# Hybrid attention and short-convolution layer on one core: the last block's output in two halves, and the preparation of weights in other places

## The reference

```
n = RMSNorm(x) ; z = n @ W_in
A: gated linear attention, 4 heads, per-head RMSNorm, times silu(g)
B: cb * conv3(cc * cu), times silu(g_conv)
h = x + [A ; B] @ W_out
h = h + sigmoid(h @ W_g + b_g) * (p @ W_ple)
out = RMSNorm(h) * final_norm_w
```

## Time and profile before

| | |
|---|---|
| three runs | 2047.91, 2048.13, 2050.92 us |
| profiled execution, its own time | 2050.24 us |
| span of its trace | 2048.4 us |
| TensorE granted clock, mean | 0.99 of full speed |
| busy: PE, DVE, ACT, POOL | 97%, 65%, 38%, 34% |
| one load of a weight matrix on SP | 2048 KB, median 8.8 us from issue to landing |
| chain that ended last, by engine | PE 87%, DVE 5%, issue 3%, ACT 2%, DMA 1% |

### The profile page before, as it was taken

The page is one execution under the profiler, slowest core; times in us unless marked ns, Lnnn a source line. Parts: engine busy times, 40 slices in busy tenths (PEclk is TensorE's granted clock), DMA queues, the critical chain, the costliest instruction groups (busy, mean ns, idle before and its releaser), DMA issues.

```text
span 2048.4 us, 28892 instructions
## 1 busy us (share of the span) xinstructions
PE 1983.6 (97%) x11266; PEld 1722.9 (84%) x11266; DVE 1338.9 (65%) x1569; ACT 782.3 (38%) x1219; POOL 689.5 (34%) x758
## 2 busy tenths in 40 slices
PE   6999999999999879999999999999999999999996
PEld 4888888888888758888888888888788999999996
DVE  4775667666654365775775775685674577777776
ACT  4354354444433323323333233223223255445543
POOL 3766666666551131231331331255551000000000
PEclk9999999999999989999999999999999999999998
DMA  6345354354446232136532137585587812222222
GB/s 228 136 161 194 135 192 179 144 200 165 161 176 279 96 108 85 67 108 249 183 110 83 60 111 259 198 297 200 191 287 285 321 58 88 93 81 86 83 83 83
DMA packets 88305, 322.84 MB, mean 158 GB/s; under 512 B 11600, under 2 KB 22272, under 8 KB 77184
## 3 DMA queue, kind: packets, MB, share of 16 engines
q1 hardware_dynamic: 55328, 185.46, 24.6%
q0 software_dynamic: 32864, 135.85, 18.3%
HBM read 193.34 MB, written 127.93 MB: 157 GB/s over the span
## 4 chain that ended last, share of the span: by engine, by line
PE 87%; DVE 5%; issue 3%; ACT 2%; DMA 1%; POOL 0%; SPq 0%; DVEq 0%; ACTq 0%; POOLq 0%
PE bank L1220 14%; PE bank L1226 14%; PE bank L1222 14%; PE bank L966 8%; PE bank L974 8%; PE bank L967 8%; PE bank L1312 5%; PE bank L1306 5%; PE bank L1308 5%; PE bank L1053 1%; PE bank L1355 1%; PE bank L1354 1%; PE bank L1353 1%; PE bank L1113 1%; PE bank L1104 1%
## 5 line engine op out<-in xcount | busy, mean ns | idle before, releaser
L1220 PE MATMUL bank<-XH,WC 128*128 128x512 f32 x1344 | 526.2, 392 | 23.4 <-DVE ccs L2031 20.1
L1222 PE MATMUL bank<-XH,WC 128*128 128x512 f32 x1344 | 524.0, 390 | 0.0
L1226 PE MATMUL bank<-XL,WC 128*128 128x512 f32 x1344 | 523.9, 390 | 0.0
L2005 DVE TENSOR_TENSOR XL<-RQ,XH 128x1024 fp32r<-128x1024 f32 x168 | 220.9, 1349 | 244.6 <-ACT XH L1598 243.6
L1220 PEld LDWEIGHTS bank<-XH,WC 128*128 128x128 f32 x1344 | 253.1, 188 | 76.9 <-issue 20.8
L1226 PEld LDWEIGHTS bank<-XL,WC 128*128 128x128 f32 x1344 | 253.0, 188 | 52.7
L1222 PEld LDWEIGHTS bank<-XH,WC 128*128 128x128 f32 x1344 | 253.2, 188 | 52.0
L1312 PE MATMUL bank<-XLg,WC 128*128 128x256 f32 x896 | 254.2, 284 | 2.8 <-DVE XLg L2243 2.8
L1306 PE MATMUL bank<-XHg,WC 128*128 128x256 f32 x896 | 253.5, 283 | 0.0
L1308 PE MATMUL bank<-XHg,WC 128*128 128x256 f32 x896 | 253.4, 283 | 0.0
L1598 ACT ACTIVATE XH<-RQ 128x1024 fp32r<-128x1024 f32 x168 | 170.7, 1053 | 194.4 <-PE bank L1226 148.1
(11 more groups left out here) (216 smaller groups left out, 3651.4 us busy)
## 6 DMA issues: line engine op xcount, KB each, us to landing
WC<-w_scratch SPq DMA_DIRECT2D x28, 2048.0 KB, 8.8
RQ<-n_scratch POOLq DMA_DIRECT2D x32, 1024.0 KB, 5.4
w_scratch<-prep_hi POOLq DMA_DIRECT2D x84, 256.0 KB, 2.3
w_scratch<-PB POOLq DMA_DIRECT2D x84, 256.0 KB, 2.3
n_scratch<-raw SPq DMA_DIRECT2D x8, 2048.0 KB, 7.1
y_scratch<-y_sb SPq DMA_DIRECT2D x64, 256.0 KB, 2.8
RQ<-y_scratch POOLq DMA_DIRECT2D x16, 1024.0 KB, 5.7
xt<-xb_dram SPq DMA_DIRECT2D x64, 256.0 KB, 5.2
```

Source lines behind the costliest of these rows:

```text
L1220: nc.tensor.matmul(bank[:], WC[:, i, q, 0, k], xh, start=(k == 0 and i in (P1, P2, P5)), stop=False, skip_group_check=True)
L1222: nc.tensor.matmul(bank[:], WC[:, i, q, 1, k], xh, start=False, stop=False, skip_group_check=True)
L1226: mm = nc.tensor.matmul(bank[:], WC[:, i, q, 0, k], xl, start=False, stop=(k == 3), skip_group_check=True)
L2005: nc.vector.tensor_tensor(XL[:, k], RQ[:, OPERAND[s % 7], 2 * h:2 * h + 2], XH[:, k].bitcast(F32), ALU.subtract).then_inc(sx_lo, 1)
```

## The change

- **First product of a gate operand (`gate_product`).** For q = 0 the eight products with the high part come first, then the wait for the low part, then the four products with the low part. Before, the wait stood behind the second product.
- **Strips.** `STRIPS_OF` puts 0, 4, 4, 4, 3, 3, 3, 3 strips in steps 0 to 7.
- **Pieces.** `GATE_SLOTS` is now (1, 1, 1), (5, 3, 0), (5, 1, 1), (2) for steps 8 to 11. Before it was (1, 1, 1), (5, 3, 1), (5, 2, 1), and nothing in step 11.
- **Wait for weights.** Before P1's matrix of the gate stage SP waits for all strips and two of the stores' counters only, and for the rest before P5's. The wait for the `W_ple` tiles ahead of it stays.
- **Block 7.** P4 comes behind the per-layer products of units 6 and 7. The mean square is made apart for the two halves of the tokens (`last_stats`: fp32 products with ones over `acc` and, for units 6 and 7, over their squares directly), `last_rms` makes `Ln` and `Exp` of 256 tokens, `last_norm` scales 8 tiles of 256 tokens, t = 1 first, and SP stores each half in four transfers.

```diff
+LAST_STAT = (0, 5)
...
+STRIPS_OF = (0, 4, 4, 4, 3, 3, 3, 3)
...
-GATE_SLOTS = {NB: (1, 1, 1), NB + 1: (5, 3, 1), NB + 2: (5, 2, 1)}
+GATE_SLOTS = {NB: (1, 1, 1), NB + 1: (5, 3, 0), NB + 2: (5, 1, 1), NB + 3: (2,)}
...
                 if i == P1:
-                    wait_prepared(sp, g // NP + 2)
-                    if g == STEPS - 1:
+                    if g < STEPS - 1:
+                        wait_prepared(sp, g // NP + 2)
+                    else:
                         sp.wait_ge(tile_stored, 16 * 2 * STRIPS)
+                        sp.wait_ge(prep_stored[2], 16 * (24 + 8))
+                        sp.wait_ge(prep_stored[5], 16 * (84 + 14))
+                if i == P5 and g == STEPS - 1:
+                    wait_prepared(sp, 4)
...
-            store_out(NB - 1, 1)
+            for n, t in enumerate((1, 0)):
+                tokens = slice(t * HT, t * HT + HT)
+                for c in range(4):
+                    m = slice(2 * c, 2 * c + 2)
+                    sp.wait_ge(out_norm, 8 * (NB - 1 + n) + 2 * c + 2)
+                    sp.dma_start(out[NB - 1, :, m, tokens], raws[(NB - 1) % 2][:, m, tokens]).then_inc(rows_stored[c], 16)
...
                 if is_conv(g):
-                    for n in range(3 * g, 3 * g + 3):
+                    for n in range(sum(STRIPS_OF[:g]), sum(STRIPS_OF[:g + 1])):
                         strip(n)
-                elif g in GATE_SLOTS:
+                else:
                     gate_parts(g, 0)
-                elif g == STEPS - 1:
+                if g == STEPS - 1:
                     for n in range(PLE_K):
                         prep_tile(n)
...
-                        if q == 0 and k == 0:
-                            pe.wait_ge(gx_lo, z + 1)
-                        mm = nc.tensor.matmul(acc_ap, WC[:, i, q, 0, k], xl, start=False, stop=(k == 3),
-                                              skip_group_check=True)
+                        if q > 0:
+                            mm = nc.tensor.matmul(acc_ap, WC[:, i, q, 0, k], XLg[:, z % 2, k], start=False, stop=(k == 3),
+                                                  skip_group_check=True)
+                    if q == 0:
+                        pe.wait_ge(gx_lo, z + 1)
+                        for k in range(4):
+                            mm = nc.tensor.matmul(acc_ap, WC[:, i, q, 0, k], XLg[:, z % 2, k], start=False, stop=(k == 3),
+                                                  skip_group_check=True)
...
-                for c, i in enumerate((P2, P5, P3, P4)):
+                for c, i in enumerate((P2, P5, P3)):
                     gate_product(b, i)
                     ple_unit(b, 2 * c)
                     ple_unit(b, 2 * c + 1)
+                if b < NB - 1:
+                    gate_product(b, P4)
+                ple_unit(b, 6)
+                ple_unit(b, 7)
+                if b == NB - 1:
+                    gate_product(b, P4)
...
+            def last_stats():
...
+                pe.wait_ge(g_acc, 6 * b + 4)
+                product(1, acc[:, 1], True, True).then_inc(out_mean, 1)
+                pe.wait_ge(g_sum, 6 * b + 5)
+                product(0, acc[:, 0], True, False)
+                pe.wait_ge(g_sq, 8 * b + 7)
+                product(0, square_place(b, 6), False, False)
+                pe.wait_ge(g_sq, 8 * b + 8)
+                product(0, square_place(b, 7), False, True).then_inc(out_mean, 1)
...
+                if b == NB - 1:
+                    gate_square(b, 4)
+                    gate_square(b, 5)
+                    sigmoid(b, 6)
+                    gate_square(b, 6)
+                    sigmoid(b, 7)
+                    nc.scalar.preload_act_table_set(LOG_EXP)
+                    last_rms(1, NB)
+                    gate_square(b, 7)
+                    last_rms(0, NB + 1)
+                    return
...
+            for n, t in enumerate((1, 0)):
+                dve.wait_ge(out_rstd, NB + n)
+                last_norm(t)
```

More of the change, by code:

```diff
@@ L1373, in out_stats, with product @@
                     wait_out_read(STAT)
[L1374 to L1378 removed]
                 pe.wait_ge(out_split, b + 1)
                 mean_of_split(STAT, total_hi[:], total_lo[:]).then_inc(out_mean, 1)
+            def last_stats():
+                b = NB - 1
+                def product(t, squares, start, stop):
+                    bank = ps[LAST_STAT[t]][:, t * HT:t * HT + HT]
+                    for j in range(2):
+                        mm = nc.tensor.matmul(bank, ones[:].bitcast(F32), squares[:, j * HT:j * HT + HT],
+                                              start=(start and j == 0), stop=(stop and j == 1))
+                    return mm
+                pe.wait_ge(g_acc, 6 * b + 4)
[6 more added lines that the diff above has]
+                product(0, square_place(b, 7), False, True).then_inc(out_mean, 1)
             pe.wait_ge(memsets, 5)
@@ L1786, in gate, with last_rms @@
                 gate_square(b, 7)
+            def last_rms(t, n):
+                tokens = slice(t * HT, t * HT + HT)
+                act.wait_ge(out_mean, n)
+                nc.scalar.activation(R_out[:, tokens], ps[LAST_STAT[t]][:, tokens], ACT.Ln, bias=eps[:],
+                                     scale=1.0 / D_MODEL).then_inc(out_root, 1)
+                act.wait_ge(out_root, n)
+                nc.scalar.activation(R_out[:, tokens], R_out[:, tokens], ACT.Exp, scale=-0.5).then_inc(out_rstd, 1)
             def out_rms(b):
@@ L2333, in gate, with last_norm @@
                 gate_total(b)
+            def last_norm(t):
+                tokens = slice(t * HT, t * HT + HT)
+                for m in range(KT):
+                    here = raws[(NB - 1) % 2][:, m, tokens]
+                    nc.vector.scalar_tensor_tensor(out=here, in0=here, scalar=vec[:, V_FIN + m:V_FIN + m + 1],
+                                                   in1=R_out[:, tokens], op0=ALU.mult, op1=ALU.mult).then_inc(out_norm, 1)
             def final_norm(b, tiles):
```

20 lines of the change are left out of this document (5 added, 15 removed).

## The result

The changed kernel takes **2019.26 us** (median of four runs, 2017.04 to 2020.20) beside 2048.58 us of the kernel before in the same session. The ratio is 0.9853, 95% interval 0.9836 to 0.9870: 1.5% faster. The range (2010.0 to 2019.5) holds it, just; the forecast itself, 2012.4, is 6.9 us too low. The profiled execution took 2019.48 us with a span of 2017.7, where before it was 2048.4: 30.7 us less.

A forecast was written before the change was run, and what follows sets the result against it. PE, busy 97% of the span, was taken as the bound; its waits and the end were to give -22.5 - 5.0 + 0.5 - 3.9 - 4.8 = -35.7 us, from 2048.13 to 2012.4 us, range 2010 to 2019.5.

The forecast's parts named there:

- Strips out of step 0: Start of step 1: T1 no longer waits behind three strips, so PE's 20.1 us wait and slow restart go, -22.5 us.
- The fourth strips in steps 1 to 3: Steps 1 to 3: one more strip takes 6.7 us of POOL, covered by 18.31 us of idle time, 0 us.
- Piece 11 behind T3: Start of step 10: T3 and DVE get through earlier, so PE's 3.2 us wait and slow restart go, -5.0 us.
- Pieces 18 and 19: Step 11: W_ple tiles end about 10.4 us later, delaying the gate stage's loads and first low part, +0.5 us.
- rival 1: Step 11 gives some back: tiles outlast their cover or loads delay the first gate operand, 3 to 9 us, 2017; chance 0.17.
- a new wait of PE at the first gate products: Start of the gate stage: a new PE wait here, or at P5 of step 11, would show the prediction wrong.
- rivals 1 and 2: Step 11 gives some back, 0.17; PE's stall at step 10's start stays, 3 to 5 us, 2017, 0.12.
- The finer wait buys nothing: Ahead of P1's gate matrix: SP stands at the W_ple tiles first, so splitting the wait for weights gains nothing.
- High products first: P6 in gate blocks 1 to 7: six more products before the low-part wait remove 0.55 us seven times, -3.9 us.
- The last block: Kernel's end: scalings of two token halves end at 2040.5 instead of 2045.3, last store landing as before, -4.8 us.
- the first went whole: Start of step 1: a rival had the 20.1 us stall go only in part, 2018 to 2030; chance 0.06.
- stores were not served one by one: Kernel's end: a rival had eight stores go one by one at 2.7 us each, 2025; chance 0.04.

The follow-up runs named there:

- the one with the pieces back: The changed kernel with GATE_SLOTS as before the change, so no pieces in step 11 and piece 11 again ahead of T3: 2011.54 us.
- the pieces are done earlier: The changed kernel with GATE_SLOTS (2, 2, 1), (6, 1, 0), (5, 2, 1), (0) for steps 8 to 11: 2014.07 us, ratio 0.9828.
- first experiment: The changed kernel with SP's wait for the W_ple tiles and the p_raw load put behind the loads of P1's, P6's and P7's matrices: 2018.67 us, ratio 0.9849.

## Why the prediction came out as it did

**Strips out of step 0: right, 1.0 us too large.** -22.5 forecast; -21.5 in the stretch, and with the strips alone as well. The stretch without the stall is 78.0 us and not 77.1: the allowance of 0.9 us for what step 0 has more than the others was too small, and a wait of 0.3 us for DVE stays in it. The fourth strips in steps 1 to 3 cost nothing: T1 of step 1 still has 10.24 us of idle time before it (forecast about 11).

**Piece 11 behind T3: right.** -5.0 forecast, -5.05 measured, and for the reason given: it is T3's lead that ends the stall. T3 came 5.1 us earlier against the mark (36.7 instead of 41.8). How much the old order costs depends on a load's landing: 5.0 to 5.8 us in four kernels, but 1.6 in the one with the pieces back.

**Pieces 18 and 19: the step that failed.** The term was +0.5 with bounds 0 and +4; it was +6.6. Its parts: POOL's own time was right (3.8 us idle before T1, forecast 1.5), the first matrix at 1534 was right, and the slack of the low part, 2.6 us, was right. T1 itself still came 1.9 us late (8.3 us behind the mark instead of 6.4), at no cost to PE, because POOL's split now lies beside two of DVE's low parts. Behind them DVE makes T4, and T1 waits for T4. The two low parts take 4.22 us here and 2.36 where the pieces are done earlier:

```profile
1528.21 4.22 DVE L2061 TENSOR_TENSOR XL<-RQ,XH 128x1024 fp32r<-128x1024 f32 x2 [8.00 <-ACT XH L1637]
...
1527.80 2.40 POOL L858 TENSOR_TENSOR tile_raw<-tile_raw,tile_hi 128x1024 f32<-128x1024 f32 x1
```

What failed is "I put the delay of the xt tiles before it at 0.7 to 4 us". The delay is 6.8: the last tile lands 52.7 us behind the mark instead of 45.9. I had counted on the queue to catch up between 1534 and 1562, but 16 DMA engines busy for 97% didn't, and most of the delay at the head of the queue reached its end (9.8 us late at the head, 6.8 at the end). 6.8 less 2.6 leaves 4.2 us, and PE's ninth product is 4.25 us late. The slow clock adds 1.5, close to the 1.8 of the other stalls, and the second wait, at P6, which the prediction didn't have, the last 0.9.

That is rival 1, which had a chance of 0.17 and a price of 3 to 9 us at 2017; the gate side of it came true, the T1 side didn't in the change, though it did as soon as the matrices went ahead (first experiment). It is also one of the signs by which the prediction called itself wrong: a new wait of PE at the first gate products. The forecast's own range ended at 2015; that the wider range holds 2019.26 is owed to the share that rivals 1 and 2 had in it, and that it does so by 0.24 us is luck, since the end of the attention stage alone moves by more.

**"The finer wait buys nothing": right in direction.** P1's matrix goes out 7.3 us behind the mark with it, 7.5 without.

**High products first: right, slightly undersized.** -4.5 against -3.9. The step between two starts was 0.55 more than the pitch, and the product behind it came another 0.1 late; a block lost 0.64.

**The last block: right, slightly undersized.** -5.2 against -4.8: the last store landed in 2.16 us, not in the 2.7 of a store twice as large. P4's new place is worth only 0.6 us of it. The rest is the split in halves; 2.0 us of that come from the eight small stores in place of four.

**The other rivals.** The second stall did not stay, the first went whole, stores were not served one by one. The forecast's span was 2048.4 less 35.7, 2012.7. With 6.1 us (6.6 less 0.5) put back, less the 0.6, 0.4 and 0.05 of the undersized terms, the 1.0 us of the strips' term and the 1.0 of an earlier end of the attention stage cancelling, the span comes to 2017.7.

## What to carry to other kernels

Work moved out of one wait has to be costed at the new place by all that stands behind it on every queue, and a full DMA queue can pass most of a delay at its head on to its end (here 6.8 of 9.8 us): read the share of the DMA engines in the stretch before assuming that a late load catches up. Before moving work later, look for idle time earlier; here it was there (14 us before T1 of step 8), and the version that used it was free of stalls from step 1 to the gate mark. And compare stretches between marks that repeat to a few hundredths, not medians, when a part far from the change moves by several us from run to run.

## What the runs showed that I had not expected

- Four stores of 512 KB, issued 0.8 us apart, queue behind each other (2.69 to 4.16 us to land); eight of 256 KB at the same spacing land in 2.2 us each.
- Four additions of two SBUF tiles on DVE take 6.95 to 10.9 us beside POOL's instructions and 2.49 while POOL is idle; four with one operand in a bank take 2.47 beside the same POOL.
- POOL's transfers of 512 KB took 8 to 10 us, where the same ones had taken 3 to 4, once SP's 2 MB loads ran beside them, with the DMA engines at no more than 0.71 of their time on average in that stretch (1513 to 1537 us, 251 GB/s).
- The attention stage ends at 684.2 to 690.0 us in thirteen profiles of kernels that don't differ in it, while those of the twelve steps behind it that have no stall repeat to 0.1 us. What moves it was not tried.
